# Layer norms of a two-block transformer kernel: running sums and shifted squares, statistics by token, three tiles at once

## The chip, the cores and the metric

The kernel is one program on one core of a Trainium2 chip, written instruction by instruction with its own semaphores. The metric is the device time of one execution in microseconds (us), less is better. The matrix engine (TensorE, PE), the vector engine (VectorE, DVE), the scalar engine (ScalarE, ACT), GpSimd (POOL) and the queue that issues most loads (SyncE, SP) each run their own instruction list and meet only at semaphores.

## The reference

Input 512 tokens by 1024 features. Block 1 has two layers. Each is a mixer (projections, compressed and windowed attention, a short convolution, output projection), a norm, a feed-forward part (dense in layer 0, eight experts in layer 1), a norm. Block 2 (a gated recurrence with attention) follows. The change is at these norms:

```
def layer_norm(x, g, b):
    xf = x.astype(jnp.float32)
    mu = jnp.mean(xf, -1, keepdims=True)
    var = jnp.mean(jnp.square(xf - mu), -1, keepdims=True)
    return ((xf - mu) * lax.rsqrt(var + LN_EPS) * g + b).astype(x.dtype)
...
    for l in range(DEPTH):
        m = hybrid_mixer(h, ...)
        h = layer_norm(ALPHA * h + m, ln1_g[l], ln1_b[l])
        if l % 2 == 0:
            f = swiglu(h, ffn_wg[l // 2], ffn_wu[l // 2], ffn_wd[l // 2])
        else:
            f = moe_swiglu(h, moe_router[l // 2], moe_wg[l // 2], moe_wu[l // 2], moe_wd[l // 2])
        h = layer_norm(ALPHA * h + f, ln2_g[l], ln2_b[l])
```

## The kernel before

**Tiles.** The state H lies feature by feature: eight tiles H[:, k, :] of 128 features by 512 tokens. A projection makes output tiles of the same shape. For precision each fp32 factor is split in a rounded head and a rest, in the activations (HH, HL) and in the weights (head, rest), and an output tile is 24 matmuls of 512 columns: head x HH, head x HL, rest x HH for each of eight k (33 matmuls where eleven k are summed, in the down projection). Weights come through a ring of three slots: SP loads raw, ACT rounds it to head (`make_head`), POOL subtracts (`split`, rest = raw - head), and PE writes tile n to bank n mod 3. Banks 3 to 7 serve everything else. Tile n+3 needs the bank and the slot of tile n. `make_head(n)` waits for the end of tile n-3.

**Norms 1 and 3** follow the output projection of mixer(0) and mixer(1); norm 2 follows the dense feed-forward part. Each one has sums over the 1024 features, which lie across partitions, so PE makes them. As the eight tiles come in, DVE adds each to H (`mixer`, `down`) and sums the H tiles in rstd (`summed`). After the last: PE multiplies the sum by a matrix of 1/1024 (`mean_of_sum`, bank 3: the mean of each token on all partitions); DVE subtracts it from all eight tiles (`centre`); ACT squares each in the two sq buffers and PE sums them (`var`, bank 4); ACT takes the root of 128x512, DVE its reciprocal, and multiplies the eight tiles; ACT applies gain and bias to H, then rounds to HH; DVE makes HL. Norm 2 also has 24 matmuls of one column (`mod_columns`) between the mean and the squares, which sum mod_sum (a vector of block 2) over partitions.

**Behind a norm**, `together` runs the first two tiles of the next projection side by side in k, since the HL tiles come one by one; the third and later tiles run alone (`tile`). After norm 2, ACT issues seven DMAs (`compression_weights`) before it takes the first tiles out of their banks (`keys`). After norm 3 the router matmuls (L1047) read H as it comes, then tokens are turned, sorted and sent to the experts. The experts stream 270 weight pieces from DRAM.

**Norm 4** in front of block 2 is a root-mean-square norm with the same `var` and `together`. Its arithmetic stays; its `together` and the gate matmuls (`lru_gates`, L1195) after each tile change.

**The first part of the feed-forward** (`gate_up(0)`, eleven pairs of tiles j) has side work: ACT issues the load of a 1 MB chunk of w_mod after UH(j) (`side_loads`), DVE reduces it in eight instructions after UL(j) (`mod_chunk`), and only then takes gu(j+1). UH(j+1), the next chunk's load and the next head wait for that on ACT.

## Time and profile before

| | us |
|---|---|
| time, median of 3 runs (lowest, highest) | 2512.21 (2508.54, 2516.76) |
| the profiled execution, its own time | 2510.85 |
| its span, first to last instruction | 2509.0 |
| PE busy | 2336.9 |
| DVE busy | 1389.2 |
| ACT busy | 1160.7 |
| POOL busy | 542.3 |

Matmuls are pipelined, so "busy" on PE is close to "has something to do", not to its peak rate. The granted clock (PEclk) is a share of full speed: 1.00 is 2.4 GHz and 0.50 is 1.2 GHz. Times inside the program are us from the start of the span. Where a single core runs, the difference between time and span, 1.85 us, lies around the program.

### The profile page before, as it was taken

Reading aid. Unit: us, or ns where it says so; the run is one execution under the profiler, and the core shown is the slowest. Engines: PE = TensorE matmul, PEld = TensorE weight load, DVE = VectorE, ACT = ScalarE, POOL = GpSimd, SP = SyncE. Lnnn points to the kernel's source line nnn. Section 1 sums busy time; section 2 is a strip of 40 time slices with the busy share of each in tenths; the row PEclk is TensorE's granted clock in tenths of the full one; section 3 lists DMA queues with packets and bytes.
Section 4 is the critical chain, followed back from the end, with each engine's and each line's share of the span. In section 5 each row is a group of like instructions: output and inputs, shape, how many; then the busy total and the mean of one; then the engine's idle time right before and its main releaser. Section 6 shows DMA issues by size and latency. Waiting matters only on the chain.

```text
span 2509.0 us, 29613 instructions
## 1 busy us (share of the span) xinstructions
PE 2336.9 (93%) x11014; PEld 1835.9 (73%) x11014; DVE 1389.2 (55%) x1920; ACT 1160.7 (46%) x1466; POOL 542.3 (22%) x230
## 2 busy tenths in 40 slices
PE   6999989899988999959999999999975999999998
PEld 5866758688867766638877887878853788877786
DVE  4277465501123377358888888888866771245332
ACT  3244342212223344257677767776744653233423
POOL 3111323434422211210000000000011344433242
PEclk9999999999989999979999999999986999999999
DMA  7211237723314211349999999999982223322232
GB/s 209 59 43 43 76 92 235 242 76 97 108 47 130 51 47 38 101 167 352 364 370 368 355 369 369 369 348 365 370 294 69 83 86 101 92 68 70 65 92 67
DMA packets 381090, 435.96 MB, mean 174 GB/s; under 512 B 12944, under 2 KB 287808, under 8 KB 380992
## 3 DMA queue, kind: packets, MB, share of 16 engines
q1 hardware_dynamic: 348772, 393.38, 46.8%
q10 hardware_dynamic: 29916, 32.88, 4.3%
q0 software_dynamic: 2304, 8.39, 0.8%
q8 instruction: 62, 1.02, 0.2%
q14 instruction: 36, 0.29, 0.0%
HBM read 410.50 MB, written 22.02 MB: 172 GB/s over the span
## 4 chain that ended last, share of the span: by engine, by line
PE 55%; issue 32%; DVE 7%; DMA 3%; ACT 3%; ACTq 1%; POOL 1%; SPq 0%; DVEq 0%; POOLq 0%
PE bank L779 19%; PE bank L783 10%; PE bank L965 5%; PE bank L1224 5%; PE bank L799 2%; DMA mod_raw<-in_w_mod_dram 2%; PE bank L865 2%; PE bank L940 2%; PE bank L1001 2%; PE bank L982 2%; DVE mod_sum L1916 1%; PE bank L829 1%; PE bank L1263 1%; PE bank L1247 1%; DVE rstd L1934 1%
## 5 line engine op out<-in xcount | busy, mean ns | idle before, releaser
L720 POOL TENSOR_TENSOR rest<-raw,head 128x1024 fp32r<-128x1024 f32 (+1 forms) x210 | 522.6, 2493 | 1117.1 <-ACT head L1362 1117.0
L2188 DVE TENSOR_TENSOR rest_m<-raw_m,head_m 128x2048 fp32r<-128x2048 f32 (+2 forms) x270 | 567.4, 2112 | 126.8 <-ACT head_m L1401 126.0
L1401 ACT ACTIVATE head_m<-raw_m 128x2048 fp32r<-128x2048 f32 (+2 forms) x270 | 477.4, 1775 | 200.3 <-DMA raw_m<-in_moe_wu_dram 72.0
L1362 ACT ACTIVATE head<-raw 128x1024 fp32r<-128x1024 f32 (+1 forms) x210 | 225.3, 1076 | 275.3 <-PE bank L783 236.9
L779 PE MATMUL bank<-HH,head 128*128 128x512 f32 x784 | 318.6, 406 | 4.0 <-ACT head L1362 4.0
L779 PE MATMUL bank<-HL,head 128*128 128x512 f32 x784 | 312.7, 399 | 0.0
L1095 PE MATMUL bank<-head_m,XH 128*128 128x512 f32 (+1 forms) x720 | 280.2, 389 | 4.4 <-DVE rest_m L2188 2.5
L1095 PE MATMUL bank<-head_m,XL 128*128 128x512 f32 (+1 forms) x720 | 271.7, 377 | 0.0
L1095 PE MATMUL bank<-rest_m,XH 128*128 128x512 f32 (+1 forms) x720 | 271.3, 377 | 0.0
L783 PE MATMUL bank<-HH,rest 128*128 128x512 f32 x784 | 198.8, 395 | 0.0
L779 PEld LDWEIGHTS bank<-HH,head 128*128 128x128 f32 x784 | 149.9, 191 | 43.2 <-ACT head L1362 4.5
L779 PEld LDWEIGHTS bank<-HL,head 128*128 128x128 f32 x784 | 149.7, 191 | 37.1 <-issue 1.7
L759 POOL DMA_INDIRECT y_back<-y_rows,idx x8 | 7.6, 946 | 768.3 <-DMA y_rows<-ys 766.1
L783 PEld LDWEIGHTS bank<-HH,rest 128*128 128x128 f32 x784 | 146.9, 187 | 36.0
L1095 PEld LDWEIGHTS bank<-head_m,XH 128*128 128x128 f32 x720 | 136.0, 189 | 32.8 <-DVE rest_m L2188 7.7
L1095 PEld LDWEIGHTS bank<-head_m,XL 128*128 128x128 f32 x720 | 136.0, 189 | 22.0
L1095 PEld LDWEIGHTS bank<-rest_m,XH 128*128 128x128 f32 x720 | 136.3, 189 | 19.1
L1103 PE MATMUL bank<-head_m,UTH 128*128 128x512 f32 x330 | 132.4, 401 | 9.3 <-DVE rest_m L2188 9.3
L1583 ACT ACTIVATE Psw<-Psw,nb 128x128 f32<-128x128 f32 (+3 forms) x128 | 71.0, 555 | 139.6 <-DVE nb L2044 139.6
L1103 PE MATMUL bank<-head_m,UTL 128*128 128x512 f32 x330 | 130.8, 396 | 0.0
L1103 PE MATMUL bank<-rest_m,UTH 128*128 128x512 f32 x330 | 130.8, 396 | 0.0
L1224 PE MATMUL bank<-HH,head 128*128 128x512 f32 x192 | 89.0, 463 | 0.0
(375 smaller groups left out, 3796.2 us busy)
## 6 DMA issues: line engine op xcount, KB each, us to landing
raw_m<-in_moe_wd_dram SPq DMA_DIRECT2D x75, 1024.0 KB, 8.4
raw_m<-in_moe_wg_dram SPq DMA_DIRECT2D x60, 1024.0 KB, 6.1
raw_m<-in_moe_wu_dram SPq DMA_DIRECT2D x60, 1024.0 KB, 7.9
raw<-in_w_in_dram SPq DMA_DIRECT2D x110, 512.0 KB, 3.9
raw_m<-in_moe_wg_dram SPq DMA_DIRECT2D x30, 768.0 KB, 6.2
raw_m<-in_moe_wu_dram SPq DMA_DIRECT2D x30, 768.0 KB, 5.1
raw<-in_w_o_dram SPq DMA_DIRECT2D x24, 512.0 KB, 4.0
mod_raw<-in_w_mod_dram ACTq DMA_DIRECT2D x12, 1024.0 KB, 6.5
```

Source lines behind the costliest of these rows:

```text
L720: pool.tensor_tensor(rest[slot][:, 0:kt, :], raw[slot][:, 0:kt, :], head[slot][:, 0:kt, :], ALU.subtract).then_inc(weights_split, 1)
L779: pe.matmul(bank[slot][:, 0:cols], head[slot][:, k, :], act[:, k, 0:cols], start=(k == 0 and act is hi), stop=False)
L783: last = pe.matmul(bank[slot][:, 0:cols], rest[slot][:, k, :], hi[:, k, 0:cols], start=False, stop=(k == kt - 1))
L799: last = pe.matmul(bank[slot][:, :], w[slot][:, k, :], act[:, k, :], start=(j == 0 and first), stop=(j == KT - 1 and final))
L965: last = pe.matmul(bank[slot][:, :], w[slot][:, k, :], x[:, k, :], start=(k == 0 and w is head and x is HH), stop=(k == KT - 1 and w is rest))
L1095: last = pe.matmul(out, x[:, kk, :], v[slot][:, k * w:(k + 1) * w], start=(kk == 0 and v is head_m and x is XH[hf]), stop=(kk == KT - 1 an ...
L1103: last = pe.matmul(bank[6 + b][:, :], x[:, c, :], v[slot][:, k * D + b * 512:k * D + b * 512 + 512], start=(c == 0 and x is UTH and v is h ...
L1224: ins = pe.matmul(bank[slot][:, :], w[slot][:, k, :], x[:, k, :], start=(k == 0 and w is head and x is HH), stop=(k == KT - 1 and w is rest))
L1362: act.activation(head[slot][:, 0:kt, :], raw[slot][:, 0:kt, :], ACT.Copy).then_inc(head_done, 1)
L1401: act.activation(head_m[slot][:, 0:width], raw_m[slot][:, 0:width], ACT.Copy).then_inc(gran_head, 1)
L1583: act.activation(Psw[:, s % 2, r, 0:w], Psw[:, s % 2, r, 0:w], ACT.Exp, bias=nb[:, s % 2, r:r + 1], scale=-1.0, accum_out=Z[:, s % 2, r:r ...
L2188: dve.tensor_tensor(rest_m[slot][:, 0:width], raw_m[slot][:, 0:width], head_m[slot][:, 0:width], ALU.subtract).then_inc(gran_split, 1)
```

## The change

The mean and the variance of norms 1 to 3 are made another way. After the third tile PE makes a shift from H tile 0 alone (`norm_shift`: a matrix of 1/128, so the mean of 128 features), DVE subtracts it from every tile as it comes, sums the tiles (rstd) and adds the squares, which ACT makes per tile (Psw or gu). After the last tile PE makes the mean and mean square of each token as four columns each (128x4 in banks 5 and 6; the sums are the stationary factor, the moving one has one column). Variance is the mean square minus the squared mean, on 128x4. Root and reciprocal are 128x4 too. Four diagonal matrices carry the result back to all partitions (bank 3), and one matmul spreads the mean (bank 4). `mod_columns` is cut in 7, 4 and 13 and put between these steps.

Then for each tile DVE subtracts and multiplies, ACT makes HH straight from it and H after that, DVE makes HL. `together` takes three tiles (two in the two output projections, in mixer(0) and in the last projection), starts with the products of HH, and takes HL one k later. `compression_weights` moves to SP, behind the fourth weight load of the mixer; for layer 1 it waits there for the end of norm 2's matmuls. The third head of a `together` is made inside the norm, after the root. One chunk of w_mod moves from the first part of the feed-forward to the down projection. In block 2 the gate matmuls come one tile later.

```diff
+        norm_ssum = {1: Psw[:, 0, 0, :], 2: gu[:, 0, :], 3: Psw[:, 0, 0, :]}
+        norm_diag = {1: Psw[:, 0, 1, :], 2: gu[:, 1, :], 3: Psw[:, 0, 1, :]}
...
+            def compression_weights(l):
+                if l == 1:
+                    products(sp, 2, N_RSTD)
+                    sp.wait_ge(x_zeroed, 16 * SLOTS)
+                for kv in range(2):
+                    sp.dma_start(W1[:, kv, :, :], a["cmp_w1"][l, kv].rearrange("(k p) n -> p k n", p=P)) \
+                      .then_inc(w1_landed, 16)
...
+                    if k == 3:
+                        compression_weights(l)
...
+            def together(n0, hi, lo, ready_hi, ready_lo, order=range(KT), count=3):
+                pe.wait_ge(head_done, n0 + count)
+                for n in range(n0, n0 + count):
...
+                def low(j):
+                    k = order[j]
+                    ready_lo(k)
+                    for n in range(n0, n0 + count):
+                        last = pe.matmul(bank[n % RING][:, :], head[n % RING][:, k, :], lo[:, k, :], start=False,
+                                         stop=(j == KT - 1))
                         if j == KT - 1:
                             last.then_inc(tile_done, 1)
+                for j, k in enumerate(order):
+                    ready_hi(k)
+                    for n in range(n0, n0 + count):
+                        pe.matmul(bank[n % RING][:, :], head[n % RING][:, k, :], hi[:, k, :], start=(j == 0), stop=False)
+                    if j == 0:
+                        pe.wait_ge(weights_split, n0 + count)
+                    for n in range(n0, n0 + count):
+                        pe.matmul(bank[n % RING][:, :], rest[n % RING][:, k, :], hi[:, k, :], start=False, stop=False)
+                    if j >= 1:
+                        low(j - 1)
+                low(KT - 1)
...
+            def norm_shift(L, n1):
+                taken(pe, n1)
+                pe.matmul(bank[3][:, :], mean_t[:, :], H[:, 0, :], start=True, stop=True).then_inc(npe_done, 1)
+            def norm_statistics(L, aside=(None, None, None)):
+                def idle(j):
+                    if aside[j]:
+                        aside[j]()
+                idle(0)
                 pe.wait_ge(sum_ready, L)
+                for t in range(ST):
+                    last = pe.matmul(bank[5][:, t:t + 1], rstd[:, t * P:(t + 1) * P], mean_w[:, 0:1], start=True,
+                                     stop=True)
+                last.then_inc(npe_done, 1)
+                pe.wait_ge(lsq_added, (KT - 1) * L)
+                for t in range(ST):
+                    last = pe.matmul(bank[6][:, t:t + 1], norm_ssum[L][:, t * P:(t + 1) * P], mean_w[:, 0:1],
+                                     start=True, stop=True)
+                last.then_inc(npe_done, 1)
+                pe.matmul(bank[4][:, :], mean_w[:, :], rstd[:, :], start=True, stop=True).then_inc(npe_done, 1)
+                idle(1)
+                for t in range(ST):
+                    pe.wait_ge(diag_ready, ST * (L - 1) + t + 1)
+                    last = pe.matmul(bank[3][:, t * P:(t + 1) * P], ones[:, :], norm_diag[L][:, t * P:(t + 1) * P],
+                                     start=True, stop=True)
+                last.then_inc(npe_done, 1)
+                idle(2)
...
+                L, n1 = 2 * l + 1, n0 + N_PROJ
+                together(n1, MH, ML, head_in, rest_in, order=[4, 5, 6, 0, 1, 2, 7, 3], count=2)
+                tile(n1 + 2, MH, ML)
+                norm_shift(L, n1)
+                for k in range(3, KT):
+                    tile(n1 + k, MH, ML)
+                norm_statistics(L)
...
-                down(DENSE_PARTS - 1)
-                mean_of_sum(2)
-                mod_columns()
-                var(2)
+                down(DENSE_PARTS - 1, last=True)
+                norm_statistics(2, (lambda: mod_columns(0, 7), lambda: mod_columns(7, 11),
+                                    lambda: mod_columns(11, N_MOD)))
...
-            for k in range(2, KT):
+            together(B2_X, HH, HL, *normed(3 * KT))
+            for k in range(3, KT):
                 tile(B2_X + k, HH, HL)
-                lru_gates(k - 2)
+                lru_gates(k - 3)
+            lru_gates(KT - 3)
...
+            def norm_tiles(L, n1, head_of):
+                for k in range(3):
+                    head_of(k)
+                act.activation(nst[:, 1, 0:1], eps[:, 0:1], ACT.Sqrt)
+                for k in range(3, KT):
+                    head_of(k)
+                    for j in range(0 if k == 3 else k - 1, k):
+                        norm_square(L, n1, j)
+                norm_square(L, n1, KT - 1)
+            def norm_out(L, g, b, row, next_head):
+                act.wait_ge(var_ready, L)
+                act.activation(nst[:, 1, :], nst[:, 0, :], ACT.Sqrt, bias=eps[:, 0:1]).then_inc(lstd_ready, 1)
+                if next_head is not None:
+                    make_head(next_head)
                 for k in range(KT):
-                    act.wait_ge(xn_ready, KT * (L - 1) + k + 1)
+                    act.wait_ge(y_ready, KT * (L - 1) + k + 1)
+                    if next_head is not None:
+                        act.activation(HH[:, k, :], H[:, k, :], ACT.Identity, bias=col(b, row + k),
+                                       scale=col(g, row + k)).then_inc(hh_ready, 1)
...
+            def norm_tiles(L, n1, scale):
+                ssum = norm_ssum[L]
+                def residual(k, by):
+                    n = n1 + k
+                    dve.wait_ge(tile_done, n + 1)
+                    if by is None:
+                        take(dve.tensor_tensor(H[:, k, :], H[:, k, :], bank[n % RING][:, :], ALU.add), n)
+                    else:
+                        take(dve.scalar_tensor_tensor(out=H[:, k, :], in0=H[:, k, :], scalar=by,
+                                                      in1=bank[n % RING][:, :], op0=ALU.mult, op1=ALU.add), n)
+                def square_added(k):
+                    dve.wait_ge(lsq_ready, KT * (L - 1) + k + 1)
+                    dve.tensor_tensor(ssum, sq[:, 0, :] if k == 1 else ssum, sq[:, k % 2, :], ALU.add) \
+                       .then_inc(lsq_added, 1)
+                    dve.wait_ge(lsq_added, (KT - 1) * (L - 1) + k)
+                for k in range(3):
+                    residual(k, scale)
+                for k in range(3):
+                    taken(dve, n1 + k)
+                products(dve, L, N_SHIFT)
+                for k in range(3):
+                    dve.tensor_tensor(H[:, k, :], H[:, k, :], bank[3][:, :], ALU.subtract).then_inc(d_ready, 1)
+                for k in range(3, KT):
+                    if scale is None:
+                        step(dve.tensor_tensor(H[:, k, :], H[:, k, :], bank[3][:, :], ALU.subtract))
+                    else:
+                        step(dve.scalar_tensor_tensor(out=H[:, k, :], in0=H[:, k, :], scalar=scale, in1=bank[3][:, :],
+                                                      op0=ALU.mult, op1=ALU.subtract))
+                    if k == 3:
+                        dve.wait_ge(d_ready, 3 * L)
+                        for j in (1, 2):
+                            step(dve.tensor_tensor(rstd[:, :], H[:, 0, :] if j == 1 else rstd[:, :], H[:, j, :], ALU.add))
+                        for j in (1, 2):
+                            square_added(j)
+                    residual(k, None)
+                    taken(dve, n1 + k)
+                    ins = dve.tensor_tensor(rstd[:, :], rstd[:, :], H[:, k, :], ALU.add)
+                    if k == KT - 1:
+                        ins.then_inc(sum_ready, 1)
+                    else:
+                        step(ins)
+                    square_added(k)
...
+            def norm_out(L, split_=True):
+                products(dve, L, N_DELTA)
+                step(dve.tensor_scalar(nst[:, 0, :], bank[5][:, 0:ST], -1.0, None, ALU.mult))
+                step(dve.tensor_tensor(nst[:, 0, :], nst[:, 0, :], bank[5][:, 0:ST], ALU.mult))
+                products(dve, L, N_SQUARE)
+                dve.tensor_tensor(nst[:, 0, :], nst[:, 0, :], bank[6][:, 0:ST], ALU.add).then_inc(var_ready, 1)
+                dve.wait_ge(lstd_ready, L)
+                step(dve.reciprocal(nst[:, 0, :], nst[:, 1, :]))
+                for t in range(ST):
+                    dve.tensor_scalar(norm_diag[L][:, t * P:(t + 1) * P], ident, nst[:, 0, t:t + 1], None, ALU.mult) \
+                       .then_inc(diag_ready, 1)
+                products(dve, L, N_SPREAD)
+                for k in range(KT + 1):
                     if k < KT:
-                        dve.tensor_tensor(H[:, k, :], H[:, k, :], rstd[:, :], ALU.mult).then_inc(xn_ready, 1)
-                    if split_ and k >= 2:
-                        dve.wait_ge(hh_ready, KT * L + k - 1)
-                        dve.tensor_tensor(HL[:, k - 2, :], H[:, k - 2, :], HH[:, k - 2, :], ALU.subtract) \
+                        step(dve.tensor_tensor(H[:, k, :], H[:, k, :], bank[4][:, :], ALU.subtract))
+                        if k == 0:
+                            products(dve, L, N_RSTD)
+                        dve.tensor_tensor(H[:, k, :], H[:, k, :], bank[3][:, :], ALU.mult).then_inc(y_ready, 1)
+                    if split_ and k >= 1:
+                        dve.wait_ge(h_ready, KT * (L - 1) + k)
+                        dve.tensor_tensor(HL[:, k - 1, :], H[:, k - 1, :], HH[:, k - 1, :], ALU.subtract) \
...
-                        if k < MOD_CHUNKS - PT + 1 and not last:
-                            mod_chunk(PT - 1 + k)
-                        if last and k >= 1:
-                            taken(dve, BASE_MIX[1] - KT + k - 1)
-                            summed(k - 1)
-                    if last:
-                        taken(dve, BASE_MIX[1] - 1)
-                        summed(KT - 1)
+                        if k < MOD_CHUNKS - PT + 2:
+                            mod_chunk(PT - 2 + k)
...
-                    if j < PT - 1:
+                    if j < PT - 2:
...
```

**DVE, from the last tile of norm 1's projection to the first HL.** Before:

```order
L1996 SCALAR_TENSOR_TENSOR H<-H,bank0 128x512
L1904 TENSOR_TENSOR rstd<-rstd,H 128x512 x2
L1930 TENSOR_TENSOR H<-H,bank3 128x512 x8
L1934 RECIPROCAL rstd<-rstd 128x512
L1944 TENSOR_TENSOR H<-H,rstd 128x512 x3
```

Of the changed kernel, the same place:

```order
L2033 SCALAR_TENSOR_TENSOR H<-H,bank3 128x512
L2011 TENSOR_TENSOR H<-H,bank0 128x512
L2043 TENSOR_TENSOR rstd<-rstd,H 128x512
L2018 TENSOR_TENSOR Psw<-Psw,sq 128x512
L2073 TENSOR_SCALAR nst<-bank5 128x4
L2074 TENSOR_TENSOR nst<-nst,bank5 128x4
L2076 TENSOR_TENSOR nst<-nst,bank6 128x4
L2078 RECIPROCAL nst<-nst 128x4
L2080 TENSOR_SCALAR Psw<-cst,nst 128x128 x4
L2085 TENSOR_TENSOR H<-H,bank4 128x512
L2088 TENSOR_TENSOR H<-H,bank3 128x512
L2085 TENSOR_TENSOR H<-H,bank4 128x512
```

Eight subtractions and a reciprocal of 128x512 went out of the stretch behind the last tile, and small instructions came in; the first four rows now stand once per tile.

**PE, from norm 2's last down tile to the first tiles of mixer(1).** Before:

```order
L783 MATMUL bank0<-UH,rest0 128x512 x11
L824 MATMUL bank3<-rstd,mean_w 128x512
L836 MATMUL bank5<-ones,mod_sum 128x1 x24
L829 MATMUL bank4<-sq,mean_w 128x512 x8
L799 MATMUL bank1<-HH,head1 128x512
L799 MATMUL bank1<-HL,head1 128x512
```

Of the changed kernel:

```order
L814 MATMUL bank0<-UH,rest0 128x512 x11
L906 MATMUL bank7<-ones,mod_sum 128x1 x7
L878 MATMUL bank5<-mean_w,rstd 128x1 x4
L883 MATMUL bank6<-mean_w,gu 128x1 x4
L886 MATMUL bank4<-rstd,mean_w 128x512
L906 MATMUL bank7<-ones,mod_sum 128x1 x4
L890 MATMUL bank3<-gu,ones 128x128 x4
L906 MATMUL bank7<-ones,mod_sum 128x1 x13
L837 MATMUL bank1<-HH,head1 128x512
L837 MATMUL bank2<-HH,head2 128x512
L837 MATMUL bank0<-HH,head0 128x512
```

The eight matmuls of squares are gone, the 24 columns stand in three groups, the last 13 ahead of the first tile, and three banks are filled at once.

**ACT, behind norm 2.** Before:

```order
L1392 ACTIVATE HH<-H 128x512
L1346 DMA W<-in_cmp_w_dram 128x16x256
L1349 DMA W<-in_cmp_w_dram 128x2x64 x2
L1346 DMA W<-in_cmp_w_dram 128x16x256
L1349 DMA W<-in_cmp_w_dram 128x2x64 x2
L1351 DMA b2row<-in_cmp_b_dram 31x64
L1539 ACTIVATE K<-bank 64x512
```

Of the changed kernel:

```order
L1495 ACTIVATE H<-H,par 128x512
L1637 ACTIVATE K<-bank 64x512
L1638 ACTIVATE K<-bank 64x512
L1643 DMA K<-K 64x512 x2
L1444 ACTIVATE head<-raw 128x1024
L1637 ACTIVATE K<-bank 64x512
```

The seven DMAs are gone from ACT; the head of the fourth tile still stands behind the first tile's copies.

## Rows read from the trace of the kernel before

**Rows 1.** Windows: length, busy PE, PEld, DVE, ACT, POOL, clock, DMA share, GB/s.

```profile
317.20:338.40 21.20, 10.33 (x18) 3.39 (x18) 12.88 (x17) 9.21 (x14) 0.00 (x0) 0.86 0.07 22
721.40:756.30 34.90, 21.82 (x67) 14.38 (x67) 16.42 (x20) 11.58 (x17) 2.36 (x1) 0.70 0.06 15
1050.80:1071.50 20.70, 11.31 (x18) 3.64 (x18) 11.81 (x15) 7.86 (x12) 0.00 (x0) 0.79 0.57 203
```

**Rows 2.** Timeline of norm 1, in order: start us, us, engine, line, operation.

```profile
317.30 0.69 DVE L1996 SCALAR_TENSOR_TENSOR H<-H,bank 128x512 f32<-128x512 f32 x1 [4.21 <-PE bank L783]
317.90 1.41 DVE L1904 TENSOR_TENSOR rstd<-rstd,H 128x512 f32<-128x512 f32 x2
319.37 1.12 PE L824 MATMUL bank<-rstd,mean_w 128*128 128x512 f32 x2 [2.18 <-DVE rstd L1904]
320.53 4.87 DVE L1930 TENSOR_TENSOR H<-H,bank 128x512 f32<-128x512 f32 x8 [1.22 <-PE bank L824]
336.11 0.81 ACT L1388 ACTIVATE H<-H,par 128x512 f32<-128x512 f32 x1 [4.14 <-DVE H L1944]
338.46 0.77 PE L799 MATMUL bank<-HH,head 128*128 128x512 f32 x1 [7.32 <-DVE HL L1947]
```

**Rows 3.** Windows behind norm 1: first 4 us, and to the pair's end.

```profile
338.40:342.40 4.00, 3.94 (x9) 3.14 (x10) 3.77 (x7) 3.93 (x6) 0.00 (x0) 0.50 0.00 0
342.40:351.40 9.00, 9.00 (x39) 7.26 (x38) 3.99 (x7) 7.12 (x10) 2.40 (x1) 0.98 0.00 0
```

**Rows 4.** Timeline of the program's last sums: columns of one, then the 128x4 root.

```profile
2499.49 0.95 PE L1318 MATMUL bank<-mean_w,rstd 128*128 128x1 f32 x8
2500.48 0.26 ACT L1850 ACTIVATE fsd<-bank,eps 128x4 f32<-128x4 f32 x1 [1.42 <-PE bank L1318]
```

**Rows 5.** Timeline of norm 2 and of the tiles behind it.

```profile
722.17 3.43 DVE L1904 TENSOR_TENSOR rstd<-rstd,H 128x512 f32<-128x512 f32 x2
722.68 2.36 POOL L720 TENSOR_TENSOR rest<-raw,head 128x1024 fp32r<-128x1024 f32 x1 [5.26 <-ACT head L1362]
...
727.52 10.24 PE L836 MATMUL bank<-ones,mod_sum 128*128 128x1 f32 x48
...
775.05 0.59 ACT L1539 ACTIVATE K<-bank 64x512 f32<-64x512 f32 x1 [11.38 <-PE bank L783]
...
777.59 1.06 ACT L1362 ACTIVATE head<-raw 128x1024 fp32r<-128x1024 f32 x1 [1.33 <-issue]
...
778.70 0.50 PE L779 MATMUL bank<-HH,head 128*128 128x512 f32 x1 [4.05 <-ACT head L1362]
```

**Rows 6.** Window over the one-column matmuls.

```profile
727.50:737.50 10.00, 10.00 (x49) 9.98 (x47) 4.87 (x8) 1.23 (x2) 0.00 (x0) 0.50 0.07 21
```

**Rows 7.** Timeline, feed-forward part: gu(0), gu(9), and the start of the down projection.

```profile
351.94 0.69 DVE L2302 TENSOR_TENSOR gu<-silu_g,bank 128x512 f32<-128x512 f32 x1 [4.04 <-PE bank L799]
...
460.82 0.68 DVE L2302 TENSOR_TENSOR gu<-silu_g,bank 128x512 f32<-128x512 f32 x1
...
464.58 0.50 PE L779 MATMUL bank<-UH,head 128*128 128x512 f32 x1 [0.75 <-ACT head L1362]
...
476.82 0.79 PE L779 MATMUL bank<-UH,head 128*128 128x512 f32 x1 [7.30 <-DVE UL L2305]
```

**Rows 8.** Chain of waits, same place: the second down tile starts.

```profile
482.74 1.45 PE bank L779 x6
```

**Rows 9.** Timeline, the router behind norm 3.

```profile
1071.58 9.52 PE L1047 MATMUL bank<-H,rw 128*8 128x512 f32 x16 [5.93 <-ACT H L1388]
```

**Rows 10.** Timeline, first matmul behind norm 4.

```profile
1923.30 0.77 PE L799 MATMUL bank<-HH,head 128*128 128x512 f32 x1 [9.35 <-DVE HL L2371]
```

**Rows 11.** Chain of waits behind it: pair, third tile, gates, fourth tile.

```profile
1940.61 3.73 PE bank L779 x16
...
1946.21 1.79 PE bank L1195 x4
1948.01 2.11 PE bank L779 x9
```

241 lines of the change are left out of this document (109 added, 132 removed).

## The prediction

> **What bounds the kernel now.** I read the slices of the span and the busy times first: PE is busy for 93% of the span, so most stages are its own work, and no change at a norm can touch that. What can move is the time in which PE waits or does work that is not a tile. The windows show it: from the last tile of a stage to the first matmul of the next lie 21.2 us at norm 1, 34.9 at norm 2 and 20.7 at norm 3 [rows 1], in which no tile runs. The timeline of norm 1 shows why: it is one chain through all engines [rows 2]. The last tile lands at 317.3; the last two additions and the mean end at 320.5; DVE then subtracts from eight tiles, ACT and PE do the squares, root and reciprocal follow, and PE starts at 338.46. A second place is the first part of the feed-forward. DVE takes gu(0) at 351.94 and gu(9) at 460.82 [rows 7], 12.1 us a pair, where PE needs 11.2 us for the 48 matmuls of a pair (39 records in 9.00 us are 0.233 each in this window [rows 3]). PE has slack for a while, then pays: 7.30 us of waiting for UL, at a cold clock after it, and the second down tile starts only at 482.74 [rows 7, 8].
>
> **Norm 1 step by step.** Let S be the end of the last tile. DVE adds it to H and to the sum: 0.60 + 0.69, so the sum is there at S+1.4 [rows 2]. ACT squares the tile meanwhile and DVE adds that by S+2.2. Four one-column matmuls took 0.95 us [rows 4], so the mean columns end at S+2.4 and the square columns at S+3.4. One small DVE addition (0.2), a root on 128x4 (0.26 [rows 4]) and a reciprocal bring it to S+4.2, four diagonals of 128x128 to S+5.1 (an estimate of 0.2 each, between a quarter of the 0.61 of a 512-column pass [rows 2] and the 0.26 of the 128x4 root). PE meanwhile spreads the mean: 1.12 us in this place before [rows 2], up to twice that if the clock has dropped. Its four 128x128 matmuls end between S+5.5 and S+7.0. Then one multiplication by DVE (4.87 us for eight from a bank, 0.61 each [rows 2]) and one pass by ACT (0.81 [rows 2]) and PE may start, since the first matmuls want HH only: S+7.2 to S+8.7, and I take 8.0, as the clock had dropped at this distance from the last tile before (0.86 mean in the window [rows 1]).
>
> The three tiles side by side are 72 matmuls. The first 4 us behind the norm held 9 of them at clock 0.50, the rest went at 0.233 [rows 3]: 9 x 0.43 + 63 x 0.233 = 18.6 us. DVE feeds them with three instructions per k, 0.61 + 0.61 + 0.69 us and some settling, 2.0 us, against 2.1 us of PE work per k, so PE sets the pace and T, the end of three tiles, is S+26.6. Before, the pair ended at 351.4, S+34.2, with one tile of 5.6 us less done.
>
> Now the feed-forward's side chain decides how much of that is kept. Its period (DMA landing, chunk, gu, UH, next DMA) does not depend on PE, so gu(9) follows gu(0) by 108.9 us as before [rows 7]. gu(0) comes at T+0.3, so gu(9) at T+109.2; the down projection started 3.8 us after gu(9) [rows 7], the first down tile is 33 matmuls, 7.7 us, and since the tenth pair has no chunk any more, UL(10) comes in time. So the second down tile starts at T+120.7 = S+147.3; before it was 482.74 - 317.2 = S+165.5. That is 18.2 us, less one shift matmul of 0.9 that PE now makes between tiles: **17.3 us**. So a PE that comes one tile ahead out of the norm loses it to the side chain, and what is really gained there is the 7.30 us wait and its cold clock.
>
> **Norm 2.** The same chain, but PE also has the 24 columns of `mod_columns`. They took 10.24 us, 0.43 each, all at clock 0.50 [rows 5, 6]; at full clock a column took 0.24 [rows 4]. The first seven fill the wait for the sum and cost nothing, being 1.7 us warm beside 1.4. The four in the middle hide beside root and diagonals. The last 13 lie on PE's path ahead of the first tile, while DVE and ACT already make HH. PE's own list from S: 7 + 4 + 4 columns warm (3.6 us), spread 1.9, 4 columns 1.7, diagonals 1.7, 13 columns 5.5: S+14.4, all cold from the spread on, because the columns kept the clock at 0.50 for 10 us before [rows 6]. All warm it would be S+9.9. I take 14.2. Plus 18.6: T is S+32.8. The fourth tile then waits for its head: ACT first takes the first tile out of its bank, issues two DMAs and rounds, 775.05 to 778.65, 3.6 us [rows 5], from half a us before T: S+36.0. Before, the fourth tile started at 778.70, S+57.3 [rows 5]. The seven DMAs whose issue lay in the 11.38 us ahead of 775.05 [rows 5] have gone to SP, where the weights of tiles five and on queue behind them; these are wanted only some 6 us after T, that is S+39, and SP, which starts at the norm's last matmul, is through by S+20 to S+23, so that is free. Gain 21.3, less 0.9: **20.4 us**. Not counted are 0 to 1.3 us for the bank of the third tile (DVE takes it only after its copies of K) and 0 to 1.8 us for a cold fourth tile, which it was before too.
>
> **Norm 3.** The router starts on the first H tile, S+7.9. DVE now needs two dependent instructions per tile, 1.35 us, and PE 0.9 to 1.7, so DVE sets the pace: the last tile at S+17.2, router done at S+18.1. Before: 1071.58 + 9.52 - 1050.8 = S+30.3 [rows 1, 9]. Gain 12.2, less 0.9: **11.3 us**. The expert stage starts from the router's result (its first weight pieces are loaded at S, all others wait for the scattered tokens), so all of this is kept.
>
> **Norm 4.** The norm is as before; PE starts one rest earlier, at 1922.5 instead of 1923.30 [rows 10]. Three tiles are done at 1941.1, then a head is late by 2.1 to 3.6 us: fourth tile at 1943.7. Before, it started at 1948.01, with 1.79 us of gates already done [rows 11]. 2.5 us, less about 1 for one more pair of gates in a row at the end: **1.5 us** (0 to 5).
>
> **DVE and POOL beside the tiles.** Each tile of the norms now brings DVE four passes instead of two, and ACT one more. The additions have both inputs in SBUF. Two of them took 3.43 us in norm 2, where POOL ran for 2.36 [rows 5], and 1.41 in norm 1, where it did not [rows 2]: one stood still until POOL was done. So a tile costs DVE 0.7 x 4 + 2.4 = 5.2 us, of 5.5 us for a tile in norms 1 and 3, 7.7 in norm 2: just hidden. The Trainium skill says in "SBUF — State Buffer", section "Who interferes with whom", that a DVE instruction with two SBUF inputs and a GpSimd instruction that reads SBUF exclude each other for the whole instruction. By that rule the trace agrees, and it reaches one step on: the scaling of the identity into diagonals can be shut out too if POOL's split of the third head starts first. That would be 2.4 us at each of norms 1 and 2. By my times the diagonals are done (S+5.1) just before that split starts (S+5.2), so I leave it out of the sum and in the range.
>
> **The sum.** 17.3 + 20.4 + 11.3 + 1.5 = 50.5 us. The profiled execution took 2510.85 us, so 2460.4; the median of the runs lies 1.4 above it: **2461 us**, 2.0% less.
>
> **Rivals.**
> 1. The clock does not drop behind the norms, as PE now has small matmuls to do there. Then norm 2 starts 4.3 us earlier and each of three togethers saves 9 x 0.19 = 1.8: 2461 - 9.7 = 2451. Against it: columns never raised the clock [rows 6]. Chance 0.15.
> 2. The side chain is not shortened as reckoned, or locks and late splits cost on the chains: the 10.5 us between 472.3 (464.58 + 7.7) and 482.74 [rows 7, 8] stay, or 2 x 2.4 for diagonals, 3.1 at norm 2's fourth tile and some 2 at each tile row add up to as much: 2472. Chance 0.25.
> 3. The change does not do what it says: the running work is not hidden. If DVE falls behind by one more lock per tile, 2.1 us for five tiles in norms 1 and 3 each, 21 us go: 2482. Rows of the tiles before show 4.21 us of DVE idle per tile [rows 2], enough for all but that second lock. Chance 0.06.
> 4. Slower than before, by one mechanism: tiles that HH and HL feed one k at a time let PE pause each k, and the clock stays at 1.2 GHz instead of recovering in 4 us. A matmul then costs 0.19 more. All four togethers at that clock cost 4 x 63 x 0.19 = 48 us, which only brings the time back to 2509; it decides for slower by 0.3% from another 60 matmuls on, two and a half tiles behind the togethers. Against it: in the pair behind norm 1 the clock was 0.98 after 4 us [rows 3]. Chance 0.04, half of it over the line.
>
> **How the numbers follow.** The forecast has 0.50, rivals as given. The range must hold 0.8: it leaves out rivals 3 and 4 and the outer part of 1 and 2. 2450 to 2474. About 0.3% is what a measurement of this kernel can tell from no change; faster by more has 0.96, within it 0.02, slower 0.02 (the two halves of rival 4).
>
> **What would show it.** In the profile after: gaps between last tile and first matmul of some 8, 14 and 8 us; no wait of PE for UL at the first down tile; a wait of some 3 us for a head behind norms 2 and 4; one-column matmuls at 0.12 us a record in the first group and 0.21 in the last. Wrong would be a PE wait for a bank inside the tiles ahead of a norm (rival 3), a clock of 0.50 beyond 4 us of the togethers (4), or a DVE diagonal of over 2 us (2).

## The result, and the profile after

The changed kernel takes 2484.22 us (median of 4 runs, 2482.89 to 2488.62), the kernel before, run beside it, 2510.38 us (4 runs, 2508.26 to 2516.76). The ratio is 0.990, with an interval of 0.988 to 0.992: 26 us less, where 50 were forecast. The profiled execution of the changed kernel has a span of 2481.1 us, against 2509.0.

The windows from the last tile ahead of a norm to the next matmul of a stage, of the changed kernel (columns as in [rows 1]):

```profile
315.40:323.90 8.50, 5.23 (x27) 3.92 (x27) 5.84 (x15) 2.86 (x5) 2.35 (x1) 0.73 0.18 54
703.80:716.40 12.60, 12.48 (x74) 11.92 (x73) 8.93 (x20) 5.58 (x9) 2.36 (x1) 0.69 0.32 105
1012.10:1020.70 8.60, 5.31 (x27) 4.00 (x28) 5.89 (x15) 1.74 (x3) 0.00 (x0) 0.80 0.88 308
```

They are 8.5, 12.6 and 8.6 us long where [rows 1] has 21.2, 34.9 and 20.7. The timeline of norm 1 after the change answers to [rows 2]:

```profile
311.49 2.55 DVE L2018 TENSOR_TENSOR Psw<-Psw,sq 128x512 f32<-128x512 f32 x1 [0.26 <-ACT sq L1471]
314.08 0.69 DVE L2033 SCALAR_TENSOR_TENSOR H<-H,bank 128x512 f32<-128x512 f32 x1
315.42 0.69 DVE L2011 TENSOR_TENSOR H<-H,bank 128x512 f32<-128x512 f32 x1 [0.65 <-PE bank L814]
...
316.88 1.05 PE L878 MATMUL bank<-mean_w,rstd 128*128 128x1 f32 x8 [1.57 <-DVE rstd L2043]
317.80 1.03 PE L883 MATMUL bank<-mean_w,Psw 128*128 128x1 f32 x8
...
319.67 0.87 DVE L2080 TENSOR_SCALAR Psw<-cst,nst 128x128 f32<-128x128 f32 x4
320.01 2.07 PE L890 MATMUL bank<-Psw,ones 128*128 128x128 f32 x8
...
322.19 0.69 DVE L2088 TENSOR_TENSOR H<-H,bank 128x512 f32<-128x512 f32 x1 [1.05 <-PE bank L890]
...
323.87 1.62 PE L837 MATMUL bank<-HH,head 128*128 128x512 f32 x3 [1.79 <-ACT HH L1493]
```

The running sums keep up with the tiles: DVE waits 0.65 us for each of the last three tiles ahead of norm 1 (304.22, 309.82 and 315.42 us), and PE has no wait for a bank there. So the norms became what they were meant to be. What became of the time is seen when the run is cut into stretches at rows that both kernels have (us; the last column is the same stretch in the profiles of the experiments that leave that part of the changed kernel alone):

| stretch | before | after | gain | elsewhere |
|---|---|---|---|---|
| start to the last tile ahead of norm 1 | 317.2 | 315.4 | 1.8 | 315.2 to 319.5 |
| from there to the second down tile | 165.3 | 148.6 | 16.7 | 146.0 to 147.8 |
| to the last tile ahead of norm 2 | 238.9 | 239.8 | -0.9 | 239.8 |
| to the fourth tile behind norm 2 | 57.3 | 35.5 | 21.8 | 33.9 to 35.6 |
| to the last tile ahead of norm 3 | 272.1 | 272.9 | -0.8 | 272.7 to 275.6 |
| to the request for the experts' tokens | 56.8 | 45.3 | 11.5 | 45.2 to 45.5 |
| expert stage, to the gathering of its rows | 763.0 | 769.7 | -6.7 | 763.5 to 771.9 |
| to the first squares matmul of norm 4 | 32.9 | 32.3 | 0.6 | 32.1 to 32.4 |
| to the first matmul behind norm 4 | 19.8 | 19.1 | 0.7 | 16.2 to 19.0 |
| to the first recurrent output tile of block 2 | 161.1 | 176.0 | **-14.9** | 174.5 to 177.3 |
| to the last pair side by side | 363.8 | 363.7 | 0.1 | 363.6 to 363.8 |
| to the end | 60.9 | 62.9 | -2.0 | 62.8 to 62.9 |

By the first squares matmul of norm 4 the changed kernel is 44.1 us ahead (1859.44 against 1903.51), on the way to the forecast. Behind norm 4 it gives back 14.9 us in one stretch, and 2.0 at the end. These are PE's waits in the changed kernel behind norm 4, 1875 to 1975 us (line waited for, us in total, times, longest):

```profile
PE bank L810 <- ACT head L1444: 8.7, 5, 1.8
PE bank L837 <- ACT HH L1783: 8.5, 1, 8.5
PE bank L1284 <- DVE XC L2544: 6.3, 1, 6.3
```

And the same stretch of the kernel before, 1920 to 2010 us:

```profile
PE bank L799 <- DVE HL L2371: 12.3, 6, 9.3
PE bank L1195 <- DVE XC L2414: 0.8, 1, 0.8
```

Without the first wait, that for the norm itself (8.5 and 9.3 us), PE waits 15.0 us in this stretch and waited 3.8 before (3.0 for HL within the pair, 0.8 for XC). That is 11.2 of the 14.9 us. Most of the rest lies right behind two of the waits, where the granted clock is 0.77 (1899.28 to 1906.68 us, the fourth tile) and 0.74 (1953.83 to 1961.40 us), against 1.00 over the third to the fifth tile of the kernel before.

The wait for a head is new, and it comes with every tile. One round of it in the timeline of the changed kernel, PE and ACT (the first line is the fourth tile; then L814 ends a tile, L1284 are the gates, L1807 takes them as R and IX, L1444 makes a head, L810 begins the next tile):

```profile
1899.28 0.50 PE L810 MATMUL bank<-HH,head 128*128 128x512 f32 x1 [1.84 <-ACT head L1444]
...
1913.95 2.03 PE L814 MATMUL bank<-HH,rest 128*128 128x512 f32 x8
1915.82 1.88 PE L1284 MATMUL bank<-XC,WA 128*128 128x512 f32 x4
...
1916.88 0.69 ACT L1807 ACTIVATE R<-bank,par 128x512 f32<-128x512 f32 x1 [5.66 <-PE bank L1284]
1917.73 0.69 ACT L1807 ACTIVATE IX<-bank,par 128x512 f32<-128x512 f32 x1 [0.17 <-PE bank L1284]
1918.32 1.05 ACT L1444 ACTIVATE head<-raw 128x1024 fp32r<-128x1024 f32 x1
...
1919.42 0.50 PE L810 MATMUL bank<-HH,head 128*128 128x512 f32 x1 [1.72 <-ACT head L1444]
```

ACT's written order has the head of tile k+3 ahead of R and IX of the gates of k, and the head of tile k+4 behind them. Before, gates k stood on PE right ahead of tile k+3, so its head was made by then. Now they stand right ahead of tile k+4, whose head ACT makes only when it has taken exactly these gates: a circle gates, R, IX, head, tile. Its rounds are 9.30 us long (tiles at 1910.12, 1919.42, 1928.72 and 1938.02), where tile and gates alone take 7.33 (tiles at 1948.01, 1955.34 and 1962.66 us in the chain of waits of the kernel before). The other new wait, 6.3 us for XC, belongs to the gates of the sixth and the seventh tile, which now stand in a row behind the last of these tiles; the experiments take it by itself.

### The profile page after: what moved, and what is told of

It reads as the page before. It is cut to its first block, busy times and chain, and to the rows that moved or that the text cites. A ratio compares the mean times of both kernels' runs of the same rounds, so it can differ in the third digit from the quotient of the medians.

```text
span 2481.1 us, 29748 instructions
## 1 busy us (share of the span) xinstructions
PE 2323.6 (94%) x11044; PEld 1833.3 (74%) x11044; DVE 1445.4 (58%) x1987; ACT 1162.0 (47%) x1469; POOL 544.6 (22%) x230
## 4 chain that ended last, share of the span: by engine, by line
PE 56%; issue 32%; DVE 6%; DMA 3%; ACT 2%; POOL 1%; ACTq 0%; DVEq 0%; SPq 0%; POOLq 0%
PE bank L810 20%; PE bank L814 10%; PE bank L1052 5%; PE bank L1314 5%; DMA mod_raw<-in_w_mod_dram 2%; PE bank L940 2%; PE bank L1027 2%; PE bank L1088 2%; PE bank L1069 2%; PE bank L837 2%; PE bank L841 1%; PE bank L829 1%; DVE mod_sum L2056 1%; ACT head L1444 1%; PE bank L1353 1%
## 5 line engine op out<-in xcount | busy, mean ns | idle before, releaser
L1444 ACT ACTIVATE head<-raw 128x1024 fp32r<-128x1024 f32 (+1 forms) x210 | 225.2, 1076 | 250.4 <-PE bank L814 197.2
L810 PE MATMUL bank<-HH,head 128*128 128x512 f32 x760 | 307.2, 404 | 15.7 <-ACT head L1444 15.7
L810 PE MATMUL bank<-HL,head 128*128 128x512 f32 x760 | 301.8, 397 | 0.0
L814 PE MATMUL bank<-HH,rest 128*128 128x512 f32 x760 | 192.6, 395 | 0.0
L810 PEld LDWEIGHTS bank<-HH,head 128*128 128x128 f32 x760 | 144.5, 190 | 58.7 <-ACT head L1444 17.7
L810 PEld LDWEIGHTS bank<-HL,head 128*128 128x128 f32 x760 | 144.3, 190 | 34.5 <-issue 0.8
L814 PEld LDWEIGHTS bank<-HH,rest 128*128 128x128 f32 x760 | 142.4, 187 | 34.9
L1314 PE MATMUL bank<-HH,head 128*128 128x512 f32 x192 | 88.8, 463 | 0.0
```

Source lines behind the costliest of these rows:

```text
L810: pe.matmul(bank[slot][:, 0:cols], head[slot][:, k, :], act[:, k, 0:cols], start=(k == 0 and act is hi), stop=False)
L814: last = pe.matmul(bank[slot][:, 0:cols], rest[slot][:, k, :], hi[:, k, 0:cols], start=False, stop=(k == kt - 1))
L1314: ins = pe.matmul(bank[slot][:, :], w[slot][:, k, :], x[:, k, :], start=(k == 0 and w is head and x is HH), stop=(k == KT - 1 and w is rest))
L1444: act.activation(head[slot][:, 0:kt, :], raw[slot][:, 0:kt, :], ACT.Copy).then_inc(head_done, 1)
```

## Experiments

Twelve kernels ran, in three groups of four; each group shares its runs of the kernel before. Single executions of one kernel differ by up to 16 us, so a difference of a few us is read from the stretches of the table, and the ratios to the kernel before say what it all comes to. Each kernel has one profile. Among kernels with the same code there, the stretches to the last tile ahead of norm 2, to the request for the tokens, to the first squares matmul of norm 4 and the last two repeat within 0.4 us; the others scatter by 2 to 4 us, and the expert stage by 8.

### Is it the moved gates? Two cuts, and the part by itself

Theory A is the circle. The rival is that three tiles side by side, or something that norm 4 inherits from the other norms (such as the state of the buffers), costs the 15 us. The first cut puts two tiles and the old place of the gates back:

```diff
-            together(B2_X, HH, HL, *normed(3 * KT))
-            for k in range(3, KT):
+            together(B2_X, HH, HL, *normed(3 * KT), count=2)
+            for k in range(2, KT):
                 tile(B2_X + k, HH, HL)
-                lru_gates(k - 3)
-            lru_gates(KT - 3)
+                lru_gates(k - 2)
```

> The changed kernel with only block 2's entry put back: two tiles side by side, then each tile followed by the gates of two tiles before. Theory A (the moved gates make a circle: gates, R and IX on ACT, then the head, then the tile, 9.30 us a tile against 7.33): tiles 7.33 us apart again, the 14.2 us that were lost come back, so about 14 us less than the changed kernel, 2470. Theory B (the loss lies in the three tiles or in something that norm 4 inherits from the other norms): tiles stay over 9 us apart or the gain is under 5 us.

Measured: 2466.2 us median, ratio 0.983 (0.981 to 0.984). The chain of waits of this kernel has the tiles 7.3 us apart, gates directly behind each and no head between:

```profile
1909.59 1.72 PE bank L1284 x4
1911.30 3.73 PE bank L810 x16
1915.03 1.86 PE bank L814 x8
1916.90 1.72 PE bank L1284 x4
1918.61 3.73 PE bank L810 x16
```

From the first matmul behind norm 4 to the first recurrent output tile it is 162.0 us (161.1 in the kernel before, 176.0 in the changed one). The bulk of the loss is back. The second cut leaves the three tiles and the gates where the change put them, and opens the circle on ACT:

```diff
                 n = B2_X + k
-                if k >= 1:
-                    heads_ahead(n, 1)
                 act.wait_ge(tile_done, n + 1)
...
                 take(act.activation(xpad[:, 3:3 + S], bank[n % RING][:, :], ACT.Copy), n)
+                if k < KT - 1:
+                    make_head(n + 3)
```

> The changed kernel, three tiles side by side and gates three tiles behind as they are, but ACT makes the head of tile k+3 right behind taking tile k, ahead of R and IX of the gates. Theory A (circle through the head): the 1.72 us of waiting for a head at each of the five tiles go, 7.4 us a tile, some 9 us less than the changed kernel, 2475; what three tiles side by side bring or cost beside that is the difference to the kernel with two. Theory B: the wait for a head goes and PE waits as long for the gates' banks or XC, no gain.

Measured: 2471.01 us, ratio 0.984 (0.982 to 0.986), the same stretch 167.3 us instead of 176.0, 8.7 less. PE's waits, 1875 to 1975 us:

```profile
PE bank L837 <- ACT HH L1783: 8.5, 1, 8.5
PE bank L1284 <- DVE XC L2544: 4.3, 1, 4.3
PE bank L810 <- ACT head L1444: 1.8, 1, 1.8
```

The one edit on ACT, with nothing moved on PE, took the waits away: of five waits for a head the first is left, and no other took their place; the tiles are 7.3 us apart. The heads' waits fell by 6.9 us, and the wait for the convolution late in the row from 6.3 to 4.3; together 8.9, the 9 expected. The third kernel is the kernel before with this part of the change and nothing else:

```diff
-            def together(n0, hi, lo, ready, order=range(KT)):
+            def together(n0, hi, lo, ready, order=range(KT), count=2):
...
-            together(B2_X, HH, HL, lambda k: pe.wait_ge(hl_ready, 3 * KT + k + 1))
-            for k in range(2, KT):
+            together(B2_X, HH, HL, lambda k: pe.wait_ge(hl_ready, 3 * KT + k + 1), count=3)
+            for k in range(3, KT):
                 tile(B2_X + k, HH, HL)
-                lru_gates(k - 2)
+                lru_gates(k - 3)
+            lru_gates(KT - 3)
```

> The kernel before with this part of the change alone: three tiles side by side behind norm 4 (in the old order within each k), gates three tiles behind. Theory A: slower than before by 9 to 14 us, tiles 9.3 us apart. Theory B (the loss needs the other norms' changes): within 3 us of before.

Measured: 2519.54 us, ratio 1.0042 (1.0025 to 1.0059), slower than before by 10.6 us; the stretch is 173.6 us against 161.1. PE's waits behind norm 4, 1918 to 2010 us:

```profile
PE bank L799 <- DVE HL L2372: 9.3, 1, 9.3
PE bank L779 <- ACT head L1363: 7.8, 5, 1.7
PE bank L1195 <- DVE XC L2415: 6.3, 1, 6.3
```

The same five waits for a head and the same 6.3 us for the convolution, without any of the other norms' changes. So the loss is not inherited from them. This kernel has the three tiles side by side as well as the moved gates; which of the two it is, a fourth kernel shows. It keeps the three tiles, makes the heads a tile earlier as in the second cut (not shown again), and spreads the last gates out:

```diff
             lru_gates(KT - 3)
-            lru_gates(KT - 2)
             tile(B2_Z, HH, HL)
+            lru_gates(KT - 2)
+            tile(B2_Z + 1, HH, HL)
             lru_gates(KT - 1)
...
```

> The changed kernel with ACT's heads a tile earlier, and the last gates of block 2 spread out: one tile of the next projection each between the gates of the sixth, seventh and eighth (before, the gates of the sixth and seventh stood in a row, and PE waited 4.3 us for the convolution there). Theory A (the rest of norm 4's loss is this row of gates, and with it filled three tiles side by side are worth the 6.3 us that their fourth tile is ahead of the kernel with two): 4 to 6 us less than with the heads alone, 2464 to 2467. Theory B (DVE's convolutions and gates, which follow at their own pace, set the end of the stage): the wait moves to a later tile, under 1.5 us less.

Measured: 2466.56 us, ratio 0.981 (0.977 to 0.985). The stretch is 161.3 us, 6.0 less than with the heads alone, within the 4 to 6 of Theory A. The wait for the convolution is gone, a new one of 1.6 us for ACT at a bank has come (PE's waits, 1880 to 1975 us):

```profile
PE bank L837 <- ACT HH L1784: 8.5, 1, 8.5
PE bank L810 <- ACT head L1445: 1.8, 1, 1.8
PE bank L810 <- ACT ZS L1827: 1.6, 1, 1.6
```

With three tiles side by side and no loss left, the rival of the three tiles is out too: the 15 us belong to the order of gates and heads, some 9 to the heads and 6 to the gates in a row. The other half of Theory A missed: it had the three tiles worth 6.3 us beside the kernel with two. They are worth 0.7 (161.3 against 162.0) and nothing beside the kernel before (161.1), both within the scatter of this stretch. With the gates moved as they were, they came with a loss of 15.

### The last pair

The new order within `together` (for each k all products with the high half, then the low half of the k before) is also used for the last pair, in which no input is late. This kernel writes the old order there:

```diff
-            together(B2_O, GH, GL, lambda k: pe.wait_ge(u2h_ready, 2 * KT + k + 1),
-                     lambda k: pe.wait_ge(u2l_ready, 2 * KT + k + 1), count=2)
...
+            for k in range(KT):
+                pe.wait_ge(u2l_ready, 2 * KT + k + 1)
+                for n in range(B2_O, B2_O + 2):
+                    slot = n % RING
+                    for w, x in ((head, GH), (head, GL), (rest, GH)):
+                        ins = pe.matmul(bank[slot][:, :], w[slot][:, k, :], x[:, k, :],
+                                        start=(k == 0 and w is head and x is GH),
+                                        stop=(k == KT - 1 and w is rest))
...
```

> The changed kernel, only the last pair side by side (the output projection of block 2) in the old order of its matmuls, head and low and rest for each k, each k from its low half. Theory A (the new order costs 1.9 us there: the pair's lead is spent waiting for H and at a lower clock): about 1.9 us less than the changed kernel, PE's wait for H back to 1.6 us. Theory B (that loss is a clock of that one execution): no difference over 0.5 us in the time from the pair's first matmul to the end.

Measured: 2478.49 us, ratio 0.988 (0.986 to 0.989). From the pair's first matmul to the end it is 61.1 us, against 62.9 in the changed kernel. That this is no accident of one execution the other profiles show: all seven with the new order there have 62.8 to 62.9, all seven with the old one 60.9 to 61.1. First the changed kernel, PE's next wait and the windows of the pair and of the 4 us behind the wait (last three columns: clock, DMA share, GB/s), then the kernel with the old order:

```profile
2431.64 0.44 PE L1382 MATMUL bank<-cst,H 128*128 128x128 f32 x2 [2.11 <-ACT H L1950]
2418.10:2429.50 11.40, 11.40 (x50) 8.86 (x48) 3.65 (x4) 3.28 (x5) 2.53 (x1) 1.00 0.29 86
2431.60:2435.60 4.00, 3.96 (x12) 3.15 (x13) 0.00 (x0) 2.07 (x3) 3.64 (x2) 0.58 0.34 103
```

```profile
2428.75 0.44 PE L1382 MATMUL bank<-cst,H 128*128 128x128 f32 x2 [1.64 <-ACT H L1961]
2415.70:2427.10 11.40, 11.40 (x49) 8.83 (x48) 4.14 (x4) 3.78 (x5) 2.52 (x1) 1.00 0.30 86
2428.70:2432.70 4.00, 3.95 (x18) 3.28 (x19) 0.00 (x0) 2.08 (x3) 3.68 (x2) 1.00 0.37 111
```

The pair is equally long. In the new order its first tile is complete only 0.47 us later, so PE waits 2.11 us for H instead of 1.64, and behind the longer wait the granted clock is 0.58 where it is 1.00 behind the shorter: 12 matmuls in 4 us instead of 18. That is 0.5 us of waiting and about 1.4 of clock. In all seven profiles with the new order the wait is 2.10 or 2.11 us and the clock behind it 0.57 to 0.67; in all seven with the old one 1.64 or 1.65 us and 1.00.

### Norm 1 and the side chain of the feed-forward

The prediction had it that the first part of the feed-forward hangs on its side chain (chunk, gu, UH), and that the gain is what this chain gives. Three kernels test it. The first puts the tenth chunk back:

```diff
-                        if k < MOD_CHUNKS - PT + 2:
-                            mod_chunk(PT - 2 + k)
+                        if k < MOD_CHUNKS - PT + 1:
+                            mod_chunk(PT - 1 + k)
...
-                    if j < PT - 2:
+                    if j < PT - 1:
                         mod_chunk(j)
```

> The changed kernel with the tenth chunk of the conditioning weights back where it was: DVE sums ten chunks in the first part of the feed-forward and none the less in the down projection. Theory A (the side chain sets the start of the down projection; a chunk costs it DVE's 9.9 us beyond what a pair takes without): the first gu to the eleventh takes 122.8 us again instead of 113.0, PE waits some 7 us for UL, the second down tile comes 8 to 10 us later, and half of what norm 1 and the first part gave is gone: about 8 us slower than the changed kernel. Theory B (the gain came from the shorter norm alone): under 2 us slower.

Measured: from the first gu to the eleventh 122.5 us instead of 112.9; from the last tile ahead of norm 1 to the second down tile 155.1 us instead of 146.0 to 148.6; PE's wait, 440 to 480 us, is that of [rows 7] again:

```profile
PE bank L810 <- DVE UL L2440: 7.3, 1, 7.3
```

The stretch says 6.5 to 9 us; the median, 2486.36 us with a ratio of 0.990 (0.986 to 0.994), too wide an interval to say more than that it is no faster. The second kernel is the opposite, the kernel before with the chunk moved and nothing else (the same lines of its `down` and `first_part`):

> The kernel before with one part of the change: the tenth chunk of the conditioning weights is summed in the down projection instead of in the first part of the feed-forward. Theory A (the side chain sets the start of the down projection, whatever the norm does): from the last tile ahead of norm 1 to the second down tile 156 to 158 us instead of 165.3, no wait for UL, about 8 us less than before. Theory B (the chunk's gain is only there because the norm became shorter): under 2 us. The expert stage, which lasted 763 and 765 us in the two profiles of this kernel's family and 765 to 772 in eight of the changed one's, is the same in both theories and gives one more value.

Measured: 2498.42 us (7 runs), ratio 0.9959 (0.994 to 0.998), 10.8 us less by the medians. From the first matmul behind norm 1 to the second down tile it is 134.5 us against 144.1, and no wait for UL is left. So of the 16.7 to 19.3 us of this stretch about half comes from one chunk that moved, and half from the shorter norm.

The third kernel takes back the third tile behind norm 1:

```diff
-                together(n0, HH, HL, *normed(KT))
-                tiles(n0 + RING, 2 * PT - RING, HH, HL)
+                together(n0, HH, HL, *normed(KT), count=2)
+                tiles(n0 + 2, 2 * PT - 2, HH, HL)
```

> The changed kernel, only behind norm 1 two tiles side by side instead of three (the third comes next by itself). Theory A (the first part of the feed-forward hangs on its side chain, which starts with the first two tiles; 113.0 us from the first gu to the eleventh): the pair is set by DVE's 1.92 us a k and ends about 24.0 us after the last tile ahead of the norm, against 25.1 (the three at full clock) to 27.6 (at a low clock) for three, so the second down tile comes 1 to 3 us earlier, though PE has one tile less done. Theory B (PE's head start counts): PE falls behind by the part of a tile that it no longer fills in, 3 to 4 us later at the second down tile.

Measured: the first gu comes 24.2 us after the last tile ahead of the norm, with three side by side 25.8 to 28.3; the second down tile after 144.5 us instead of 146.0 to 148.6. Theory A holds, with 1.5 to 4 us: doing less work at this place gets the stage done sooner, since the chain waits for the first two tiles only. The pair took 15.3 us here, at a granted clock of 1.00, and in the three kernels of "All together", which also have it, again 15.3 us, at clocks from 0.50 to 1.00: DVE sets its pace, with 1.92 us a k. (By the runs: 2477.31 us, ratio 0.987, 0.983 to 0.991.)

That three side by side end at such different times (17.1 to 19.6 us behind their first matmul) is the clock. The first window of 4.2 us behind norm 1, in the changed kernel and then in the kernel with the heads moved, which up to there is the same program:

```profile
323.80:328.00 4.20, 4.13 (x10) 3.29 (x11) 3.86 (x7) 3.54 (x5) 0.00 (x0) 0.50 0.44 125
```

```profile
323.80:328.00 4.20, 4.13 (x18) 3.24 (x19) 3.86 (x7) 3.53 (x5) 0.00 (x0) 1.00 0.42 124
```

### The columns of norm 2

```diff
                 norm_statistics(2, (lambda: mod_columns(0, 7), lambda: mod_columns(7, 11),
-                                    lambda: mod_columns(11, N_MOD)))
+                                    None))
...
                 together(n0, HH, HL, *normed(KT * 2 * l), count=first)
+                if l == 1:
+                    mod_columns(11, N_MOD)
```

> The changed kernel, with the last 13 of the 24 column matmuls of norm 2 moved from ahead of the three tiles to behind them, where PE waits 3.2 us for a head. Theory A (these columns, 5.4 us at a granted clock of 0.5, lie on the path): the first matmul 3.8 us earlier (HH is ready then), the columns behind the three tiles take some 1.6 us at full clock and hide in the wait for the head, the fourth tile 4 to 6.5 us earlier, the time 4 to 6.5 us less than the changed kernel's. Theory B (a rival: the clock or DVE sets the end of the three tiles anyway): under 2 us.

Measured: 2477.52 us, ratio 0.986 (0.982 to 0.990). In the timeline of PE the three tiles start earlier and the columns stand behind them, at 0.11 us a record:

```profile
714.77 1.62 PE L837 MATMUL bank<-HH,head 128*128 128x512 f32 x3 [1.79 <-ACT HH L1494]
...
732.99 2.96 PE L906 MATMUL bank<-ones,mod_sum 128*128 128x1 f32 x26
...
736.36 0.50 PE L810 MATMUL bank<-HH,head 128*128 128x512 f32 x1 [0.41 <-ACT head L1445]
```

The fourth tile starts 32.2 us after the last tile ahead of the norm, against 35.5: 3.3 us, less than the 4 to 6.5 expected. Even this is at the upper end: in one profile with the columns ahead (that of the kernel with two tiles behind norm 1) it starts after 33.9, and in one with them behind (that of the last kernel below) after 33.8. PE began 1.6 to 3.5 us earlier than in the executions with the columns ahead (10.6 us after the last tile, against 12.2 to 14.0), and the columns took 3.0 us, not 1.6, which still fits into the wait for the head.

### All together

Four edits of those shown above in one kernel: heads a tile earlier with the last gates spread out, the last pair in its old order, two tiles behind norm 1, the columns behind the three tiles.

> The changed kernel with four edits together: block 2's entry with the heads a tile earlier and the last gates spread out, the last pair in its old order, two tiles behind norm 1, the last 13 columns behind the three tiles of norm 2. If the parts add up as each was seen alone: 14 from block 2's entry, 1.9 from the last pair, 1.4 to 4 from the pair behind norm 1, 3.3 from the columns, some 21 us less than the changed kernel, 2460 to 2464. If they overlap (each one's wait is another's cover), 2465 to 2470.

Measured: 2461.47 us, ratio 0.981 (0.979 to 0.984). The stretches add up (behind norm 4 161.2, to the end 60.9, second down tile after 144.8, fourth tile of norm 2 after 32.1), and the median lies where the sum of the parts put it. Two kernels add one thing each. In one, PE fills its waits in norms 1 and 2:

```diff
+            def fill_in(count):
+                for _ in range(count):
+                    pe.matmul(bank[7][:, P:2 * P], ones[:, :], mean_w[:, :], start=True, stop=True)
...
+                norm_statistics(L, (lambda: fill_in(4), lambda: fill_in(3), lambda: fill_in(4)) if l == 0
+                                else (None, None, None))
...
+                norm_statistics(2, (lambda: (mod_columns(0, 7), fill_in(2)), lambda: (mod_columns(7, 11), fill_in(1)),
+                                    lambda: fill_in(4)))
```

> The same four edits, and small matmuls of 128 columns whose result nobody reads, put where PE waits in norms 1 and 2 (11 and 7 of them). Theory A (the clock behind a norm falls because PE stands still or makes one-column matmuls there): the granted clock of the first 4 us behind norms 1 and 2 is 1.00, not 0.50 to 0.65, and the norms end no later: 0 to 3 us less than without them. Theory B (the clock falls all the same, by what went before): still 0.50 to 0.65 behind norm 2, no gain, or a loss of up to 2 us where a filling matmul delays a needed one.

Measured: 2459.4 us, ratio 0.980 (0.977 to 0.983). Windows of 4 us behind norm 1 and behind norm 2 (the first begins 1.0 us ahead of the first matmul):

```profile
324.90:328.90 4.00, 2.94 (x12) 1.72 (x10) 3.66 (x7) 3.28 (x5) 0.00 (x0) 1.00 0.46 135
715.00:719.00 4.00, 3.98 (x15) 3.27 (x16) 3.66 (x7) 3.34 (x5) 0.00 (x0) 0.84 1.05 349
```

The clock is 1.00 and 0.84, where the kernel without the filling has 0.71 (from 0.4 us ahead of the first matmul) and 0.50. But no time came of it: the first gu comes 25.1 us after the last tile (24.5 without), the fourth tile of norm 2 after 32.4 (32.1), and the first gu to the eleventh took 114.5 us where the other kernels based on the changed one, but for that with the chunk put back, have 112.9 to 113.0. The pair behind norm 1 goes at DVE's pace, and its first matmul comes 0.7 us later than without the fillings. At norm 2 the first matmul comes 11.9 us after the last tile, against 9.6; but it does so in the next kernel too, which has no fillings, so that is not theirs. As one execution each, and with 1.00 seen behind norm 1 without filling too, this does not settle what makes the clock fall. The other kernel makes the fourth tile's head ahead of the copies of K:

```diff
                     take(act.activation(K4[64:128, kind, 1, :], bank[n % RING][64:128, :], ACT.Copy), n)
+                    if l == 1 and kind == 0:
+                        make_head(n0 + 3)
...
```

> The same four edits, and behind norm 2 ACT makes the fourth tile's head right after it has emptied the first tile's bank, ahead of the issue of the two copies of K. Theory A (this head sets the fourth tile): it starts 1.1 to 2 us earlier after the end of the three tiles, and the time is that much less. Theory B (the K copies, now issued 1.1 us later, are waited for by DVE further on): no gain by the end of the mixer.

Measured: 2453.08 us (2452.39 to 2459.82), ratio 0.979 (0.976 to 0.981), the fastest of all, 56 us under the kernel before. Yet the edit itself did nothing:

```profile
730.14 3.44 PE L906 MATMUL bank<-ones,mod_sum 128*128 128x1 f32 x26
...
731.11 1.06 ACT L1457 ACTIVATE head<-raw 128x1024 fp32r<-128x1024 f32 x1
...
733.45 0.77 PE L810 MATMUL bank<-HH,head 128*128 128x512 f32 x1
```

The head is ready at 732.2, and PE is still at the columns that were put there to fill the wait: 3.3 us from their start to the tile, where it was 3.4 with the late head. The two edits share one cover, and Theory A is out. In its profile the fourth tile starts 33.8 us after the last tile ahead of the norm, later than without the edit (32.1): at norm 2 PE began 2.2 us later, with a mean granted clock of 0.59 in the norm against 0.73. What this median has over that of the kernel without the edit (8.4 us) is not explained by it; the two profiled executions are only 1.7 us apart (spans of 2451.7 and 2453.4).

### The expert stage

From the request for the tokens to the gathering of the rows it took 763.0 us before and 769.7 after, and no part of the change touches it. In the 14 profiles it took 763.0, 765.1 and 765.3 us in the kernel before and its two variants, and 763.5 to 771.9 in the other eleven, of which three lie under 765. The same program up to there took 766.2 once and 771.9 once. So most of the 6.7 us is the scatter of single executions; whether a mean of some 3 us (767.7 against 764.5) is due to the change three profiles on one side cannot say. It stays open.

## Why the forecast was wrong, step by step

- **Norm 1 and side chain** (forecast 17.3): right. PE starts 8.5 us after the last tile (8.0 forecast), the second down tile comes after 148.6 us (147.3), in other executions after 146.0 to 147.8. The shift matmul of this norm lies ahead of it, in the stretch from the start, and is too small to see there; those of norms 2 and 3 show as 239.8 against 238.9 and 272.9 against 272.1. The three tiles took 19.6 us in this execution (18.6 forecast) and 17.1 to 18.6 in the others, by the clock. That PE's head start is lost to the side chain was right as a mechanism, but not thought to its end: it says that the third tile is in the way, which the kernel with two confirmed.
- **Norm 2** (20.4): right, with two misses that cancel in part, which is luck. PE starts after 12.6 us (14.2), since the clock fell later than forecast (the spread of the mean took 1.10 us, not 1.9), and the three tiles took 19.6 us (18.6). The fourth tile comes after 35.5 (36.0), and it waits 3.22 us for its head, as forecast. The 13 columns on the path were seen; that they could stand in this very wait was not.
- **Norm 3** (11.3): right. The router starts after 8.6 us (7.9) and ends after 18.8 (18.1); 11.5 us were gained up to the request for the tokens. That "all of this is kept" holds but for the scatter of the expert stage.
- **Norm 4** (1.5): the step that failed. The fourth tile does come as forecast: 39.8 us after the first squares matmul, against 44.5 before, 4.7 us earlier, and the forecast had 4.3. There the working stopped, with one more pair of gates at the end as the only thing behind it. It named the head that is late behind the three tiles, but took it for a wait that occurs once. It did not follow what PE's next gates release on ACT and what stands behind that in ACT's order: five waits for a head, 8.7 us, where it had one of 2.1 to 3.6. And it put about 1 us on the further pair of gates in a row, which waited 6.3 us for the convolution (0.8 before), and which cost 6.0 by the kernel that spread them. The measured term is -14.2 us (0.7 - 14.9; -13.0 in the mean over the five kernels with this part as it is), 15.7 us away from the forecast, of the 23 between forecast and result; the last pair and the expert stage hold most of the rest.
- **DVE and locks**: right. The addition of the square stands still until POOL is done (2.55 us for 0.69), and DVE's 4.95 us a tile (5.60 less the wait of 0.65) fit into 5.60; 5.2 of 5.5 were forecast. The diagonals were not shut out: four took 0.87 us. The Trainium skill says in "SBUF — State Buffer", section "Who interferes with whom", that a DVE instruction with two SBUF inputs and a GpSimd instruction that reads SBUF contend for one shared port pair, which is an exclusive lock. The rows of 2.55 us agree. For the diagonals no run here tests it: POOL's split began at 320.45, 0.8 us behind the first of them, when the last was all but done.
- **The last pair**, not in the sum and so taken as free (0): its new order cost 1.8 to 2.0 us, in every profile that has it.
- **What would show it**: no wait for UL at the first down tile, columns at 0.12 us a record ahead of the norm (1.62 us for 14) and at 0.21 in the last group (5.54 for 26), gaps of 8.5, 12.6 and 8.6 us for 8, 14 and 8: all near the forecast. That list had nothing on the tiles behind the fourth at norm 4, the same gap as in the working.
- **The start**, taken as 0: the 1.8 us of the table are within the scatter of 315.2 to 319.5, so 0 was right.
- **Rivals**: the first (the clock does not drop) came true in part: behind norm 1 it was 0.50, 0.64 or 1.00 in executions of the same code. This was good for up to 2.6 us, not for 9.7. The second gave a time (2472) by way of a side chain that was not shortened; it was shortened, and nothing of its mechanism occurred. Falling behind (the third) and a clock that stays low (the fourth) did not occur. None of the rivals had the gates of norm 4 in it. With two tiles there, and all else as it is, the kernel takes 2466 us, inside the range of the forecast.
- **Two slips of arithmetic**, neither of which decides anything: 39 records in 9.00 us are 0.231 each, not 0.233, and 2460.4 plus 1.4 is 2461.8, which rounds to 2462 and not 2461.

## What to carry to other kernels

When work is moved by one place in the order of one engine, follow the loop for two rounds and not for one: ask what the moved work releases on the next engine, what stands behind that there, and who waits for it. A circle costs its gap in every round, here 2 us times four. And ahead of a chain that waits for the first two tiles only, a third tile side by side was a delay and no head start.

## What the runs showed of the hardware

- Behind the same 8.5 us of norm 1 (PE busy for 5.2 us of them) the granted clock of the next 4 us was 0.50 in one execution and 1.00 in another, and three tiles took 2.6 us longer for it. At the last pair it was 0.57 to 0.67 behind a wait of 2.1 us and 1.00 behind one of 1.64 or 1.65, and there the 14 profiles split by the order that is written, without exception.
- One-column matmuls take 0.11 us a record (2.96 us for 26) behind three full tiles, and 0.21 (5.54 for 26) in the norm, behind other small ones.
- Two tiles side by side at DVE's pace took 15.3 us behind norm 1 whether the clock of their first 4 us was 0.50 or 1.00; three side by side, at PE's pace, took 19.6 or 17.1.
- The expert stage, which moves 353 to 356 GB/s in the mean through the DMA queues, scatters by 8 us in 770 between profiles (by 5.7 us among five with the same program up to there), more than any other stretch of the table.
